# Both halves of the transposed attention weights wait for both copies: a changed wait on TensorE in a two-layer hybrid kernel

## The reference

```
def block_attention(q, keys, vals):
    ...
    def one_block(qblk):
        s = jnp.einsum('bqkgd,bskd->bkgqs', qblk, k32) * scale
        p = jax.nn.softmax(s, axis=-1)
        return jnp.einsum('bkgqs,bskd->bqkgd', p, v32)
```

## Time and profile before

| | |
|---|---|
| Median of three runs | 1982.6 us |
| Profiled execution, its own time | 1983.4 us |
| Its span, first to last instruction | 1981.4 us |
| TensorE busy | 1824.9 us (92%), 14896 matmuls |
| VectorE busy | 654.0 us (33%) |
| ScalarE busy | 375.9 us (19%) |
| GpSimd busy | 201.0 us (10%) |
| Mean granted TensorE clock | 0.962 of full speed |
| Moved by DMA | 526.48 MB, mean 266 GB/s |

### The profile page before, as it was taken

One profiled execution on the slowest core, in us unless ns is written; L12 is line 12 of the kernel. 1 busy time (PEld: TensorE's weight loads), 2 busy tenths in 40 slices (PEclk: granted clock), 3 DMA queues, 4 the chain that ended last, 5 costly groups with the idle time before them and its releaser, 6 DMA issues. The chain is left out here.

```text
span 1981.4 us, 34559 instructions
## 1 busy us (share of the span) xinstructions
PE 1824.9 (92%) x14896; PEld 868.2 (44%) x14896; DVE 654.0 (33%) x1364; ACT 375.9 (19%) x896; POOL 201.0 (10%) x275
## 2 busy tenths in 40 slices
PE   5999989938999999999769999999399999999996
PEld 1465645422434343434334666554134444444443
DVE  2335884251212121212133558843511212121211
ACT  2224552110101010101022256421100000000000
POOL 1014200000000000101010241000001010100000
PEclk8999999968999999999889999999699999999998
DMA  9750023226999999999975301131389999999993
GB/s 386 284 217 1 1 104 130 83 113 265 381 400 400 403 403 404 401 405 402 379 279 205 128 1 46 59 149 64 120 314 385 405 392 409 394 410 394 413 395 107
DMA packets 56199, 526.48 MB, mean 266 GB/s; under 512 B 12046, under 2 KB 13694, under 8 KB 26142
## 3 DMA queue, kind: packets, MB, share of 16 engines
q1 hardware_dynamic: 48462, 498.81, 62.4%
q0 software_dynamic: 6336, 21.63, 4.5%
q10 hardware_dynamic: 1344, 5.24, 0.7%
HBM read 503.91 MB, written 24.38 MB: 267 GB/s over the span
## 5 line engine op out<-in xcount | busy, mean ns | idle before, releaser
L554 PE MATMUL PS<-arena,xe 128*32 128x512 f32 x6144 | 674.0, 598 | 3.8 <-DVE xe L1356 3.8
L554 PEld LDWEIGHTS PS<-arena,xe 128*32 128x32 f32 x6144 | 196.9, 111 | 457.4 <-issue 453.1
L578 PE MATMUL PS<-arena,hdT 128*32 128x512 f32 x1536 | 268.6, 600 | 14.4 <-DMA arena<-w_exp 14.4
L1367 DVE TENSOR_TENSOR RA<-RA,PS 96x512 f32<-96x512 f32 (+2 forms) x96 | 63.2, 684 | 649.3 <-ACT RA L1070 646.7
L580 PE MATMUL PS<-arena,hdT 128*32 128x256 f32 x1024 | 266.3, 383 | 0.0
L633 PE MATMUL PS<-arena,RB 128*128 128x512 f32 (+1 forms) x480 | 183.5, 530 | 0.0
L583 PE MATMUL PS<-arena,hdT 128*32 128x256 f32 x1536 | 156.8, 381 | 0.0
L584 PE MATMUL PS<-arena,hdT 128*32 128x256 f32 x512 | 153.2, 381 | 0.0
L1070 ACT ACTIVATE RA<-PS 96x512 f32<-96x512 f32 x32 | 19.0, 593 | 690.7 <-PE PS L554 690.7
L975 PE MATMUL PS<-arena,RB 128*128 128x512 f32 x320 | 138.9, 593 | 0.0
L580 PEld LDWEIGHTS PS<-arena,hdT 128*32 128x32 f32 x1024 | 110.8, 111 | 27.6 <-issue 0.9
(11 more groups left out here) (269 smaller groups left out, 1800.7 us busy)
## 6 DMA issues: line engine op xcount, KB each, us to landing
arena<-w_exp SPq DMA_DIRECT2D x192, 2048.0 KB, 13.0
arena<-ada_rest SPq DMA_DIRECT2D x16, 2048.0 KB, 7.7
ada<-ada_first SPq DMA_DIRECT2D x8, 2048.0 KB, 23.7
arena<-w_in SPq DMA_DIRECT2D x4, 2048.0 KB, 22.4
arena<-w_out SPq DMA_DIRECT2D x2, 4096.0 KB, 12.9
arena<-w_in SPq DMA_DIRECT2D x4, 1536.0 KB, 25.9
RC<-x_res SPq DMA_DIRECT2D x2, 2560.0 KB, 10.8
x_res<-RC SPq DMA_DIRECT2D x10, 512.0 KB, 2.6
```

Source lines behind the costliest of these rows:

```text
L554: last = mm(PS[GRP * q:GRP * (q + 1), c * 512:(c + 1) * 512], xe[:, k, GRP * grp:GRP * (grp + 1)], w[:, col_, :], start=(k == 0), stop=(k ...
L578: mm(PS[GRP * q:GRP * (q + 1), 1536:2048], tok(q), w[:, 0:512], start=first, **flags)
L1367: V.tensor_tensor(h_, h_, up, ALU.mult).then_inc(hm_rdy.sem, 1)
```

## The change

The second wait of `turn` no longer depends on the half. Before every T0(u) and every T1(u) with u of 1 or more, TensorE now waits for copy B(u-1) and for copy A(u-1).

```diff
                     pe.wait_ge(p_rdy.sem, p_rdy.at(l, 2 * u + g + 1))
                     if u:
-                        s = (pTA_rdy, pTB_rdy)[g]
-                        pe.wait_ge(s.sem, s.at(l, u))
+                        pe.wait_ge(pTB_rdy.sem, pTB_rdy.at(l, u))
+                        pe.wait_ge(pTA_rdy.sem, pTA_rdy.at(l, u))
                     for i in range(4):
                         o = (4 + g) * 512 + i * P
                         last = nc.tensor.transpose(PS[:, o:o + P], probs[:, u % 2, g, i * P:(i + 1) * P], ident[:, :])
```

## The result

| | before | changed |
|---|---|---|
| Median, five runs each | 1983.4 us | 1996.06 us |
| Range of the runs | 1981.51 to 1987.13 | 1993.56 to 2000.49 |
| Profiled execution, its own time | 1983.4 us | 1995.96 us |
| Its span | 1981.4 us | 1993.9 us |
| TensorE busy | 1824.9 us | 1824.8 us |

The ratio is 1.0064, with a 95% interval of 1.0047 to 1.0083: the changed kernel is slower. TensorE does the same work in the same busy time, so in sum all that was added is idle time.

A forecast was written before the change was run, and what follows sets the result against it. A ring of TensorE, VectorE and ScalarE, 3.98 us long and closed by the second exponential, was taken as the bound. 4.80 + 0.53 + 0.58 + 0.24 = 6.15 us a layer, 12.3 in two, on 1982.6 gave 1994.9 us; range 1991.0 to 2000.5.

The forecast's parts named there:

- the clock rival: Longer TensorE pauses in rounds 4 and 5 make its clock fall: 4.6 us more, 16.9 in all, 1999.5 us; chance 0.13.
- T1's wait for copy A costs nothing: T1's added wait: copy A precedes copy B on VectorE; 51 ns for one more wait is hidden behind Q's 1.35 us.
- Copy B holds T0, and T0 holds the scores: T0's added wait moves T0(5) from 269.65 to 270.45 and Q(6), queued behind it, from 270.43 to 271.03.
- 0.60 us in each of 16 rounds: Rounds closed by the exponentials, no four value products before T0: 0.60 us each, eight units, 4.80 us a layer.
- 0.53 us for unit 1: First unit of a layer: after copy B(0), Q(2) comes at 255.08 instead of 254.55, 0.53 us.
- 0.58 us for unit 16: Last unit, no scores behind T0: T0(16) gets ready at 317.53, T1(16) comes 0.58 us later.
- 0.04 us behind four value products: Units 6, 7, 10, 11, 14 and 15: T0 ready at 274.42 against 274.38, 0.04 us each, 0.24 us a layer.
- the Trainium skill's rule on pulling weights ahead: T0's weights lose their early load behind value products: 0.14 us for 12 units, 1.7 us, making 14.0 instead of 12.3.
- The delay is taken back behind the loop: Rival at the loop's end: a wait 6.15 us long in each layer absorbs the loss, leaving 1982.6 us; chance 0.03.
- Q passes T0: Rival on TensorE: Q(u+1) passes waiting transposes, the ring stays 3.98 us, 1982.6 us; chance 0.04, shared with nothing happening.
- What would show it: Signs: L877 waiting for DVE L1616, scores 4.5 to 4.7 us apart, loops about 6 us longer, later stages unchanged.
- the ring: Attention loop: ScalarE waits for maxima, transposes for exponentials, maxima for scores; 3.98 us long, forecast to become 4.58.

## Why the prediction was right

The forecast was 1994.9 us, 12.3 above the kernel before; 1996.06 was measured, a loss of 12.7 against the 1983.4 us of five runs. The mechanism was right. That the sizes agree so well is partly luck: in the profiled execution the wait itself is worth 10.9 us, the clock in the loops added 4.0, and the rest of the span was 2.4 shorter. The two other comparisons with T0's wait in place gave 15.2 us (T0's wait alone) and 16.6 (the changed kernel again); the last is nearer to the clock rival's 16.9 than to 12.3. By its steps:

- *T1's wait for copy A costs nothing.* Shown: ratio 0.9998 with it alone.
- *Copy B holds T0, and T0 holds the scores.* Shown from four sides: T0's wait alone brings it all, an earlier report shrinks the round by 0.33 us, putting the scores ahead of T0 brings 3.97 us back, and naming copy B alone keeps it.
- *0.60 us in each of 16 rounds.* Measured 0.57, in eight rounds of each layer. The handover was taken as 0.12 us and is 0.07 to 0.08 in this form of wait, where the instruction has already begun with copy A.
- *0.53 us for unit 1.* The kernel with T0's wait alone has Q(1) to Q(2) of layer 0 at 6.32 instead of 5.83 us, 0.49, ahead of any fall of the clock.
- *0.58 us for unit 16.* From Q(16) to line 935 it is 6.22 instead of 5.82 us, 0.40.
- *0.04 us behind four value products.* Measured 0. With the shorter handover copy B gets there just in time. By the Trainium skill's rule on pulling weights ahead ("TensorE: Matmul & The Clock Gate", "Step-by-step: what each phase is for") T0's load would have lost its head start there, 1.7 us in all at the 0.14 us of the earlier trace rows. The trace shows none of it: T0's load now begins 0.07 us behind the copy, and the scores follow 0.59 us behind that load, as they did before.
- The sum with a clock of 1.00 is 8 × 0.57 + 0.49 + 0.40 = 5.45 us a layer, 10.9 us in all, 1.4 less than forecast.
- *The clock rival* was put aside at 0.13, and is partly true. A granted clock under 1.00 in rounds 2 to 5 had been named as a sign of being wrong, and it came: 0.50 from 254 to 257 us. Of the 14.9 us by which the two loops grew in the profiled execution, 14.9 - 10.9 = 4.0 are the clock: one fall in the middle of layer 1's loop, 6.15 - 4.54 = 1.6 us, and a spell of 1.2 GHz in the first rounds of layer 0, where the kernel before had none. There Q(1) to Q(3) took 3.14 us more, of which 0.49 + 0.57 = 1.06 are the waits, so 2.1 are the clock; in layer 1, where both kernels ran partly at 1.2 GHz, 0.3 are. The spell in layer 0 began at about 253.7 us, ahead of T0(1), the first instruction that the change can delay, so its beginning isn't due to the change; whether its length is, no run shows. The loops grew as much (14.9 to 15.0 us) when the changed kernel was profiled again and with T0's wait alone. The span still grew by only 12.5 us, because it was 2.4 shorter outside the loops, and 1.9 of these come from the higher clock behind layer 0's loop, which either kernel can have.
- *The delay is taken back behind the loop* and *Q passes T0* are refuted: the loss is there in full with T0's wait, the stretch behind the loop takes 126.6 or about 128.5 us by its clock, not by the length of the loop, and with the scores ahead of T0 the rounds are 3.97 us again and 3.7 us of loss are left.
- *What would show it:* the list of waits was to name VectorE's line 1616. It didn't; it kept naming ScalarE. The timeline and the record of the wait instruction did show it. The loops were to be about 6 us longer and were 7.5 and 7.4, by the clock. All later stages were to keep their lengths; the one behind layer 0's loop was 1.9 us shorter, by the clock too.

## What to carry to other kernels

On an in-order engine, a wait costs what is queued behind the waiting instruction, not what the instruction itself is worth. Before a wait is widened "to be safe", look at whether the awaited work ends before the wait that is already there: here copy B ended 0.68 us after T0 used to start and had been off every chain until then. If the wait must stay, move the work that the ring needs ahead of it. And look at the clock too: here it fell more often behind the longer pauses, and that cost up to 1.6 us each time.

A profile that names a releaser infers it. Here it put T0's wait down to ScalarE; comparing the starts and ends of the instructions themselves named copy B.

## What the runs showed of the hardware

A wait for two semaphores let the weights load 0.07 to 0.08 us after the copy's end, one for a single semaphore 0.12 us, with otherwise the same list; both were one instruction in the trace. With two, that instruction begins when the first semaphore is there (3.05 us before the end, in T0(4)) and ends 0.045 us behind the second copy; with one, it begins 0.04 us behind the copy and takes 51 ns. So its recorded length is no measure of how long the engine stood.

TensorE's clock fell in the first rounds of at least one layer in every profiled execution that left the pauses there empty; in the kernel before, TensorE was busy 0.97 of 3.00 us just ahead of it. With nineteen transposes whose results nobody reads in these pauses it was 1.00 in both layers, in the one execution profiled.
